# Up to seven more landing places for weight loads in idle parts of the arena, and modulation loads that begin two gate blocks earlier

## What is computed

```
h = rms_norm(x); proj = h @ w_in                 # attention, HGRN2 and two gates
y_attn = sliding_window_attention(...); y_hgrn = hgrn2_recurrence(...)
merged = sigmoid(gate_a) * (y_attn @ w_attn_branch) + sigmoid(gate_b) * (y_hgrn @ w_hgrn_branch)
x = x + rms_norm(merged @ w_out)
gate, up = split(rms_norm(x) @ w_gate_up)
x = x + rms_norm((silu(gate) * up) @ w_down)
x = x + rms_norm((p @ w_ple_proj) * sigmoid(rms_norm(x) @ w_ple_gate))
for l in 0, 1:                                   # second block
    shift, scale, gate = split(silu(c) @ w_ada[l] + b_ada[l])     # the modulation
    h = layernorm(x) * (1 + scale) + shift; p = h @ w_in_2[l]
    y = concat(fourier_mix(...), mla_attention(...)) @ w_out_2[l]
    x = layernorm(alpha * x + gate * y) * g + b
```

## Time and profile before

| | us |
|---|---|
| median of three runs | 2358.62 (2352.24 to 2359.35) |
| the profiled execution | 2350.27 |
| its span, first to last instruction | 2348.2 |
| TensorE matmul busy | 2236.2 |
| TensorE weight loads busy | 1849.5 |
| DVE busy | 1511.5 |
| ScalarE busy | 1107.2 |
| mean granted TensorE clock | 0.985 of full |
| moved by DMA | 500.64 MB, mean 213 GB/s |

### The profile page before, as it was taken

The page is one execution under the profiler, slowest core; times in us unless marked ns, Lnnn a source line. Parts: engine busy times, 40 slices in busy tenths (PEclk is TensorE's granted clock), DMA queues, the critical chain, the costliest instruction groups (busy, mean ns, idle before and its releaser), DMA issues. The chain is left out here.

```text
span 2348.2 us, 27105 instructions
## 1 busy us (share of the span) xinstructions
PE 2236.2 (95%) x10514; PEld 1849.5 (79%) x10514; DVE 1511.5 (64%) x1883; ACT 1107.2 (47%) x1541; POOL 40.7 (2%) x66
## 2 busy tenths in 40 slices
PE   8999999999898999999999999997999997999997
PEld 6788888887676777777787777786888885788886
DVE  5665467757766777667777777765545556545556
ACT  5466455443334433444433334575545544545543
POOL 1000000000000000000000000000000000000000
PEclk9999999999999999999999999998999998999999
DMA  6543654368875888888888888773544474544463
GB/s 222 184 136 126 197 171 153 112 205 299 277 257 203 289 291 278 282 292 289 289 287 279 287 292 284 257 239 117 155 148 138 146 256 135 162 135 142 145 239 137
DMA packets 232768, 500.64 MB, mean 213 GB/s; under 512 B 15728, under 2 KB 24224, under 8 KB 231488
## 3 DMA queue, kind: packets, MB, share of 16 engines
q1 hardware_dynamic: 229168, 483.53, 62.8%
q0 software_dynamic: 3328, 14.88, 1.8%
q10 hardware_dynamic: 144, 0.51, 0.1%
HBM read 496.74 MB, written 2.12 MB: 212 GB/s over the span
## 5 line engine op out<-in xcount | busy, mean ns | idle before, releaser
L234 DVE TENSOR_TENSOR wl<-raw,wh 128x1024 fp32r<-128x1024 f32 (+2 forms) x696 | 835.8, 1208 | 583.7 <-ACT wh L230 578.0
L230 ACT ACTIVATE wh<-raw 128x1024 fp32r<-128x1024 f32 (+2 forms) x696 | 723.6, 1048 | 877.3 <-PE bank L213 297.7
L213 PE MATMUL bank<-wh,hh 128*128 128x512 f32 (+1 forms) x1616 | 642.9, 398 | 45.1 <-DVE wl L234 24.3
L213 PE MATMUL bank<-wh,hl 128*128 128x512 f32 (+1 forms) x1616 | 628.8, 389 | 0.0
L213 PE MATMUL bank<-wl,hh 128*128 128x512 f32 (+1 forms) x1616 | 628.6, 389 | 0.0
L213 PE MATMUL bank<-wh,ah 128*128 128x512 f32 (+1 forms) x1168 | 460.5, 394 | 18.5 <-DVE wl L234 15.6
L213 PE MATMUL bank<-wh,al 128*128 128x512 f32 (+1 forms) x1168 | 453.1, 388 | 0.0
L213 PE MATMUL bank<-wl,ah 128*128 128x512 f32 (+1 forms) x1168 | 453.1, 388 | 0.0
L213 PEld LDWEIGHTS bank<-wh,hh 128*128 128x128 f32 x1616 | 306.1, 189 | 118.6 <-DVE wl L234 37.1
L213 PEld LDWEIGHTS bank<-wh,hl 128*128 128x128 f32 x1616 | 305.9, 189 | 63.4
L213 PEld LDWEIGHTS bank<-wl,hh 128*128 128x128 f32 x1616 | 306.5, 190 | 58.1
(11 more groups left out here) (110 smaller groups left out, 976.7 us busy)
## 6 DMA issues: line engine op xcount, KB each, us to landing
raw<-in_w_in SPq DMA_DIRECT2D x264, 512.0 KB, 3.9
raw<-in_w_ada SPq DMA_DIRECT2D x192, 512.0 KB, 4.9
raw<-in_w_gate_up SPq DMA_DIRECT2D x176, 512.0 KB, 4.9
raw<-in_w_out SPq DMA_DIRECT2D x96, 512.0 KB, 4.8
raw<-in_w_down SPq DMA_DIRECT2D x88, 512.0 KB, 5.3
raw<-in_w_ple_gate SPq DMA_DIRECT2D x32, 512.0 KB, 4.5
raw<-in_w_attn_branch SPq DMA_DIRECT2D x16, 512.0 KB, 5.3
raw<-in_w_hgrn_branch SPq DMA_DIRECT2D x16, 512.0 KB, 5.6
```

What stands on the lines that cost most here:

```text
L213: return put("pe", lambda e: e.matmul(o, l, r, start=start, stop=stop_, skip_group_check=skip), w, sig, size(r) / 2400.0 * (4 if r.dtype = ...
L230: return e.activation(o, i, f, scale=scale, **k)
L234: return put(eng, lambda e: e.tensor_tensor(o, a, b, op), w, cost=vcost(eng, o))
```

## The change

The mixing also takes the items of the last two `gates` blocks as hosts, so that there are 328 of them (16 more items, all but the first four of the new order are hosts as before). The fixed ring of landing places becomes a queue, `raws`: an item takes the place at its head and puts it back at its end with the token of its last reader. Further places are lent to it with `lend_raw` and taken back with `end_raw`, which gives the tokens of the last readers:

- at the seventh `gates` block, six places at 8, 12, 16, 20, 24 and 28 of the arena, free from the snapshot taken there;
- at the first evacuation of `wo`, 16 to 28 are taken back (YR is written from there on) and five at 40, 44, 48, 52 and 60 are given, free from a snapshot taken there;
- before the first `gate`, 8 and 12 are taken back (U_);
- before `pproj`, the other five are taken back (E_).

So there are 4, 10, 11, 9 and 4 places. Each has its own semaphore. The writers of YR, U_ and E_ wait for the tokens of the places taken back.

```diff
-    mixing = [n for n, b in enumerate(blocks) if b[0] in ("wa", "wh", "wo", "gate", "up", "down")]
+    gates = [n for n, b in enumerate(blocks) if b[0] == "gates"]
+    mixing = gates[6:] + [n for n, b in enumerate(blocks) if b[0] in ("wa", "wh", "wo", "gate", "up", "down")]
...
-        raw_rel = []
+        raws = deque((RAW[:, i, :], f"w{i}", None) for i in range(NRAW))
...
+        def lend_raw(places, rel):
+
+            for o in places:
+                raws.append((kb(o, 4), f"r{o}", list(rel)))
+
+        def end_raw(places):
+
+            toks, keep = [], [r for r in raws if r[1] not in [f"r{o}" for o in places]]
+            for r in raws:
+                if r[1] in [f"r{o}" for o in places]:
+                    toks += r[2]
+            raws.clear()
+            raws.extend(keep)
+            return toks
...
-            slot = i % NRAW
-            rel = raw_rel[i - NRAW] if i >= NRAW else None
+            buf_, key, rel = raws.popleft()
...
-                raw = RAW[:, slot, 0:kk * nw]
-                t = dma("sp", raw.rearrange("p (c n) -> p c n", c=kk), src, f"w{slot}", [rel])
+                raw = buf_[:, 0:kk * nw]
+                t = dma("sp", raw.rearrange("p (c n) -> p c n", c=kk), src, key, [rel])
...
-                raw_rel.append(tl)
+                raws.append((buf_, key, [tl]))
...
                 g_rel[0] = now()
+                lend_raw((8, 12, 16, 20, 24, 28), g_rel[0])
...
+        y_rel = []
+
         def ev_post(acc, tok, done, n):
-            rel = now() if n == 0 else None
+            if n == 0:
+                y_rel.extend(end_raw((16, 20, 24, 28)))
+                y_rel.extend(now())
+                lend_raw((40, 44, 48, 52, 60), y_rel)
+            rel = y_rel
...
-        g_free, u_free = [[], []], [[], []]
+        g_free, u_free = [[], []], [end_raw((8, 12)) for _ in range(2)]
...
+        e_rel = end_raw((40, 44, 48, 52, 60))

         def ev_p(acc, tok, done, n):
             for m in range(2):
-                t = cp(E_[:, m, n * 512:(n + 1) * 512], acc[m][:, :], tok, eng="act")
+                t = cp(E_[:, m, n * 512:(n + 1) * 512], acc[m][:, :], tok, e_rel, eng="act")
```

More of the change, by code:

```diff
@@ L550, in take_item @@
                 src = WORK[f"w_ada_2@{l}"][k * P:(k + 1) * P, c * 1024:(c + 1) * 1024]
-                raw = RAW[:, slot, :]
-                t = dma("sp", raw, src, f"w{slot}", [rel])
+                raw = buf_
+                t = dma("sp", raw, src, key, [rel])
                 buf = (ada_n[0] // 16) % 2
```

## The result

| | before | after |
|---|---|---|
| median, us | 2358.79 (2352.24 to 2359.35, 4 runs) | 2281.77 (2280.95 to 2289.61, 4 runs) |
| ratio | | 0.9687, 95% interval 0.966 to 0.9714 |
| profiled execution, us | 2350.27 | 2281.50 |
| its span, us | 2348.2 | 2279.6 |

The change makes the kernel 77 us faster by the medians and 68.6 by the spans of the profiled executions.

The account below looks back on a forecast made before the run. A ring of four landing places was taken to bound the kernel through TensorE's gaps, 77 us. Gains of 54 less 1 and 1 gave 52 us, 2298 profiled; with the median 8 above, 2307 us, range 2290 to 2343.

Parts of the forecast that it names:

- a ring: Blocks `wa` to `down`: four landing places, each freed only by its last reader, are at their limit; 77 us lost.
- The turn: Mean time a landing place is taken per load: 6.8 us, so an item per 2.75 us where TensorE needs 2.72.
- The signs named in advance: From 770 us: ScalarE's load wait below 70 us, landings over 5 us, PEld share near 0.815, 290 to 300 GB/s.
- (1): More landing places from the seventh gate block to `pproj`: gains 34.8 + 17.6 + 1.6 = 54 us.
- The late operand of `wo`: At 634.75 us, first `hh` halves behind a copy that waited 4.35 us for a load; said to go too.
- (2): Modulation loads begin in the last two gate blocks: about 7 move before 500 us, hidden; benefit already in the sum.
- (3): New waits on snapshots, at `wo` evacuation, `gate` and `pproj`: 1 us taken for `pproj`'s copy, snapshots 0.
- (4): Planner may place side work elsewhere between matmuls: -4 to +4 us, taken as 0, with 1 us for jitter.
- A: Rival, chance 0.2: DMA engines are the bound, not the number of places; spread over 2326 to 2350 us.
- B: Rival, chance 0.05: TensorE's gaps come from DVE's order of work; 10 us gain at most, 2349 to 2358.
- C: Rival, chance 0.04: slower, snapshot met late at seventh gate block and first `wo` evacuation; up to 44 us, 2349 to 2393.
- D: Rival, chance 0.08: all TensorE gaps but 7 us go; 70 us gain, 2289 us.

Follow-up runs that it names:

- e3: Kernel after with one place lent instead of six and five (5 places from the seventh gate block, 6 briefly around `wo`): 2283.14 us, ratio 0.9691.
- e5: Kernel before, four places, the 192 modulation loads left out, DVE's sums kept at full length over a constant: 2282.85 us, ratio 0.9692.
- e11: Kernel after with two lent places and one more 512 KB load for every sixth item of `gate`, `up` and `down`: 2284.62 us, ratio 0.971.
- e12: Kernel after with two lent places and one more 512 KB load for every third item of `gate`, `up` and `down`: 2296.41 us, ratio 0.9762.
- e15: Kernel after with two more places (24, 28) from the program's start to the blocks that write V: 2286.13 us, ratio 0.97.
- e2: Kernel after with the modulation loads mixed in as before (312 hosts), so the places alone: 2285.44 us, ratio 0.9702.
- e4: Kernel after with two places lent instead of six and five (6, then 8 around `wo`, then 6): 2282.96 us, ratio 0.9692.
- e1: Kernel before with only the modulation loads begun in the last two gate blocks, still four places: 2330.45 us, ratio 0.9895.
- e8: Kernel after with lent places put at the head of the queue, so the very next load waits for the snapshot: 2285.27 us, ratio 0.971.
- e13: Kernel before, four places, all 328 items of `wa` to `down` as hosts, none before them: 2337.24 us, ratio 0.9922.
- e14: Kernel before, four places, 312 hosts, each modulation load shifted by half a step against the weight items: 2361.82 us, ratio 1.0026.

## Why the prediction was right in kind and short in size

**The bound.** "So it is a ring: four places, each freed only by the last reader." Right: one more place gives all the gain (e3), leaving the modulation loads out of the ring does too (e5), and neither the DMA engines (e11, e12) nor DVE's sums (e5) bind. The turn was put too short, 6.8 us where the rate shows 7.3: the ring was not 1% but some 8% behind TensorE's pace. The signs named in advance came, but for one: the weight loads' share was to be near 0.815 in the long stretch, and it is 0.830, the share without gaps.

**(1) What stays: the step that failed.** I took 77 us as lost and let 7.0 + 11 + 4 + 1 us of it stay. Measured: 7.2 for the residual, as forecast, then 0, 0.1 and 1.3. The 11 and most of the 4 were taken from 100 to 500 us, where "the ring is long enough", at 1.4 us per 100; the 1 of the last 50 us had no row. But the 3.77 us of gaps of 100 to 500 are three, and each has side work in front of it. Those of 163.34 and 467.53 us, 1.96 and 0.71 us long, end on a `wl` that stood behind side work on DVE; that of 203.63, 1.11 us, ends on an operand of the side work itself. The first of them in the kernel before, from the timelines of TensorE (152 to 164 us) and of DVE (150 to 164):

```profile
163.34 0.50 PE L213 MATMUL bank<-wh,hh 128*128 128x512 f32 x1 [1.96 <-DVE wl L234]
...
158.20 3.94 DVE L234 TENSOR_TENSOR arena<-arena 128x512 f32<-128x512 f32 x6
162.07 2.35 DVE L234 TENSOR_TENSOR wl<-raw,wh 128x1024 fp32r<-128x1024 f32 x2
```

In e15, which has two more places there, the same gap stands at the same length (TensorE, 155 to 168 us):

```profile
165.29 0.59 PE L214 MATMUL bank<-wh,hh 128*128 128x512 f32 x1 [1.96 <-DVE wl L235]
```

So places have nothing to do with it, and the long stretch has neither attention nor recurrence beside it. The row 250 to 300 in the earlier trace rows, 50.00 of 50, said as much; it was the better neighbour of the long stretch. Forecast to stay 23.0 us, measured 8.6: this is 14.4 us of the miss. The late operand of `wo` went, as said. Fuller DVE did not matter: it is busy 520 of 690 us, and TensorE never waits for it there.

**(2) The early start.** Priced at nothing beyond "it is in the sum already". Beside enough places that is about right (e2: 70 us without it, 73 to 74 by the ratio with it). But the step missed what fewer loads per item are worth while the ring is short: alone it gives 25 us. It did not move the time forecast, since the places take the whole loss anyway.

**(3) and (4) New waits and the planner.** Two microseconds were set aside and, as far as an account good to some 2 us can tell, none was spent: 68.4 of the 68.6 us by which the spans differ are the gaps' own. The snapshot wait is real (6.8 us) and covered.

**The 8 us of the median.** The sum was made against the profiled 2350.27 us and gave 2298; I then kept the 8 us by which the median of three runs stood above it. The kernel after has no such offset (profiled 2281.50, median 2281.77). Of the 25 us by which the forecast was high, 14.4 + 2 are the terms above, and the rest, some 9, this offset. Part of it was chance. In the comparisons with the experiments, runs of the kernel before lie between 2346.6 and 2364.9 us, and their medians (7 to 17 runs) between 2353.87 and 2355.73, 3 to 5 us under the 2358.62. Its runs do spread more than those of e3 and e4, which lie within 4 us and 1 us of each other. That a ring at its limit hands each slower landing on to the end would explain this; it is only argued, and e1's four runs, with the ring still short, lie within 2.2 us. The one run of the kernel after that is 8 us off, 2289.61, has a granted clock of 0.984, and the other three 0.988; the two slower runs of e15 show the same, in kernels where TensorE has no gap in the long stretch.

**The rivals.** A (0.2) fell by e11 and e12, B by e5, C's wait was found and was harmless (e8). D, "all gaps but 7 us go", is what happened, and it had 0.08. Had the nearest stretch been read for what its gaps were, D's 70 us would have been the forecast: 2289, still 7 us high by the offset.

## What to carry to other kernels

Before carrying a leftover from one stretch to another, ask what its gaps wait for; gaps of other work don't tell what a mended stretch keeps. When the queue that issues loads waits only for places while the consumer waits for landings, count the turn of a place (landing, each reader, each wait between) against the pace asked for: if the ring is behind by some per cent, one more place can be worth the whole loss (73 us here), and further places are margin. Fewer loads through it gave back only a part: 18 us for 1.9% thinner ones, 42 us for 33 of 520 left out. A DMA share of 0.86 is no ceiling by itself; ask for more and see whether the rate rises.

## What the runs showed of the hardware that was not expected

Loads of 512 KB from one queue reached 376 GB/s over 50 us and 352 over 670 us on this one core, with landings of 6.3 us in the median against 5.0 at 287 GB/s: the landing time grew by a quarter for a rate 23% higher. DVE's subtraction took no longer beside them: 1226 ns in the median in e12, 1225 in the kernel before.

With the places at their limit, 1.9% thinner loads were worth 18 us (e13), though no load had left the blocks; a shift of the pattern's phase moved the time by 6 us (e14), a part of which can be the clock. With the added places the thinning is worth 4 us at most (e2 against after).

In kernels without gaps in the long stretch the time follows the granted clock: the runs of after, e3, e4, e8 and e15 with a mean of 0.987 to 0.989 took 2280.4 to 2284.1 us, those with 0.984 took 2289.4 to 2290.3. In e15's profiled execution the clock is lower at the start, 0.95, 0.98 and 0.97 in the first three hundreds of us for 0.97, 1.00 and 1.00 in after. e14's shows the same 0.95, 0.98 and 0.97, and its code there is that of the kernel before, which has 0.97, 1.00 and 1.00. So the change in e15 need not be the cause.
